# First pair of feed forward chunks multiplied with the residual stream times its channel scale, the norm factor and the shift put in behind the products

## The reference

```python
def _rmsnorm(x, g):
    xf = x.astype(jnp.float32)
    y = xf * lax.rsqrt(jnp.mean(xf * xf, axis=-1, keepdims=True) + EPS)
    return (y * g.astype(jnp.float32)).astype(x.dtype)
...
def _swiglu(h, w1, w3, w2):
    return (jax.nn.silu(h @ w1) * (h @ w3)) @ w2
...
        x = x + g1 * _mixer(h, w_in[l], b_in[l], s5_a_re[l], s5_a_im[l], s5_log_dt[l],
...
        h = _rmsnorm(x, norm2_g[l]) * (1.0 + sc2) + sh2
        x = x + g2 * _swiglu(h, ffn_w1[l], ffn_w3[l], ffn_w2[l])
```

## Time and profile before

| | us |
|---|---|
| median of 3 runs | 864.96 |
| lowest and highest run | 862.87 and 865.06 |
| the profiled execution | 865.76 |
| its span in the trace | 864.0 |
| PE busy in the span | 837.9 |
| mean granted clock | 0.991 of full speed |

### The profile page before, as it was taken

How to read it: one execution, slowest core, us unless ns; L and a number is a source line. 1 busy time by engine, 2 the same in 40 slices (tenths; PEclk the granted TensorE clock), 3 DMA queues, 4 the chain that set the end, 5 groups by cost and what they waited for, 6 DMA issues and landing times.

```text
span 864.0 us, 10537 instructions
## 1 busy us (share of the span) xinstructions
PE 837.9 (97%) x3932; PEld 677.0 (78%) x3932; DVE 442.3 (51%) x713; ACT 322.5 (37%) x475; POOL 45.6 (5%) x74
## 2 busy tenths in 40 slices
PE   6989999999999899999999999999999999999996
PEld 3668888877887677787888788888888888888886
DVE  6789876246679755326863454333333333323222
ACT  5635444433223444342334543333333332222231
POOL 5300000000000000000002100000000000000110
PEclk9999999999999999999999999999999999999999
...
GB/s 359 255 82 97 74 74 74 86 164 270 247 292 171 49 50 74 50 55 165 97 77 120 72 97 98 97 96 96 94 93 96 92 96 88 110 86 92 107 68 97
DMA packets 149372, 100.67 MB, mean 117 GB/s; under 512 B 11072, under 2 KB 142552, under 8 KB 148312
## 3 DMA queue, kind: packets, MB, share of 16 engines
...
## 4 chain that ended last, share of the span: by engine, by line
PE 87%; DVE 5%; DMA 3%; ACT 2%; issue 1%; SPq 1%; DVEq 0%; ACTq 0%
PE bank L1699 26%; PE bank L1701 25%; PE bank L1700 25%; DMA raw<-in_w_in 3%; PE bank L1846 1%; PE bank L1942 1%; PE bank L1866 1%; PE bank L1877 1%; DVE wlo L1188 1%; PE bank L1921 1%; PE bank L1967 1%; PE bank L1933 1%; ACT whi L698 1%; PE bank L1918 0%; PE bank L1818 0%
## 5 line engine op out<-in xcount | busy, mean ns | idle before, releaser
L1699 PE MATMUL bank<-h_lo,whi 128*128 128x512 f32 x712 | 286.3, 402 | 3.4 <-DVE wlo L1188 2.5
L1700 PE MATMUL bank<-h_hi,whi 128*128 128x512 f32 x712 | 279.2, 392 | 0.0
L1701 PE MATMUL bank<-h_hi,wlo 128*128 128x512 f32 x712 | 279.0, 392 | 0.0
L1699 PEld LDWEIGHTS bank<-h_lo,whi 128*128 128x128 f32 x712 | 135.0, 190 | 37.2 <-issue 6.8
L1701 PEld LDWEIGHTS bank<-h_hi,wlo 128*128 128x128 f32 x712 | 135.0, 190 | 29.1
L1700 PEld LDWEIGHTS bank<-h_hi,whi 128*128 128x128 f32 x712 | 135.1, 190 | 28.1 <-issue 1.2
L698 ACT ACTIVATE whi<-raw 128x1024 fp32r<-128x1024 f32 x60 | 63.4, 1058 | 169.5 <-PE bank L1701 124.6
L1188 DVE TENSOR_TENSOR wlo<-raw,whi 128x1024 fp32r<-128x1024 f32 x60 | 73.3, 1223 | 100.3 <-ACT whi L698 100.2
L1701 PE MATMUL bank<-a_hi,wlo 128*128 128x512 f32 x176 | 68.5, 389 | 0.0
L1699 PE MATMUL bank<-a_lo,whi 128*128 128x512 f32 x176 | 68.5, 389 | 0.0
L1700 PE MATMUL bank<-a_hi,whi 128*128 128x512 f32 x176 | 68.5, 389 | 0.0
...
## 6 DMA issues: line engine op xcount, KB each, us to landing
raw<-in_ffn_w SPq DMA_DIRECT2D x60, 512.0 KB, 3.8
raw<-in_w_in SPq DMA_DIRECT2D x44, 512.0 KB, 4.0
slab<-in_mod_w SPq DMA_DIRECT2D x32, 512.0 KB, 5.8
...
raw<-in_w_out SPq DMA_DIRECT2D x8, 512.0 KB, 3.6
...
xtok<-in_x SPq DMA_DIRECT2D x4, 512.0 KB, 5.2
```

The source lines that it names most:

```text
L1699: mm(dst, w_h, m_l, start=first, stop=False)
L1700: mm(dst, w_h, m_h, start=False, stop=False)
L1701: return mm(dst, w_l, m_h, start=False, stop=last)
```

## The change

The first pair of chunks, F0 and F1, is no longer multiplied with h2. Since h2 = (x1 * gs2) * rstd + shift, the product is W^T h2 = (W^T z) * rstd + W^T shift, with z = x1 * gs2, which needs no norm factor. So:

- ACT writes z in high part (z_hi) and in full (x1g) right behind each square, and DVE its low part (z_lo, `scaled_lo`).
- DVE makes W^T shift for F0 and F1: eight linked multiply-adds per chunk from the raw weights (sacc, `shift_times_w`), before the weights are split in place; PE sums it over partitions with a product of one column each, and DVE copies the result (bcol).
- PE multiplies F0 and F1 with z in banks 4 and 7, k by k. Both groups of `square_columns` go in after k = 2, the two shift columns and the four products that spread rstd after k = 4. All keep_clock products of this passage are gone.
- rstd is spread in bank 5 and ACT copies it to SBUF (rbs); htmp and the new zt (the pair's results times rstd) read it there. Silu gets the shift as its bias, the w3 side gets it in the product.
- F2 and F3 are multiplied as a pair, k by k, with h2, in banks 2 and 3. F3's split by ACT and DVE moves up into the loop over k. F4 to F7 are split ahead of the loops of ACT and DVE, which start one round later.

```diff
+            def scaled(n):
+                if n == 0:
+                    act.wait_ge(s_gs2, 1)
+                    act.wait_ge(s_x2t, KB)
+                    act.wait_ge(s_up, 3 * KB)
+                A(z_hi[:, n], xT[:, n], ACT.Copy, scale=gs2[:, n:n + 1]).then_inc(s_zhi, 1)
+                A(x1g[:, n], xT[:, n], ACT.Copy, scale=gs2[:, n:n + 1]).then_inc(s_x1g, 1)
...
+                act.wait_ge(s_col, n + 1)
                 if n == KB - 1:
-                    act.wait_ge(w_mm, S_F1 - 1)
-                    for s in range(S_F1, S_F1 + 2):
-                        act.wait_ge(w_loaded[s % 4], SLOT_LOADS[s])
-                        A(whi4[:, s % 4], raw[:, s % 4], ACT.Copy).then_inc(w_hi, 1)
-                act.wait_ge(s_col, n + 1)
+                    scaled(n)
                 act.wait_ge(s_sqa, n - 2)
                 A(sq[:, n % 2], xT[:, n], ACT.Square).then_inc(s_sq, 1)
-                scaled(n)
+                if n < KB - 1:
+                    scaled(n)
+                if n == KB - 3:
+                    hi4(S_F1, S_F1 - 2)
+                    hi4(S_F1 + 1, S_F1 - 1)
             act.wait_ge(s_sqmm, 1)
             A(rstd[:], ps[5][:, 0:NT], ACT.Sqrt, bias=epst[:, 0:1], scale=1.0 / D).then_inc(s_std, 1)
-
-            act.wait_ge(w_loaded[(S_F1 + 2) % 4], SLOT_LOADS[S_F1 + 2])
-            A(whi4[:, (S_F1 + 2) % 4], raw[:, (S_F1 + 2) % 4], ACT.Copy).then_inc(w_hi, 1)
+            hi4(S_F1 + 2, S_F1)
+            act.wait_ge(s_rb, 1)
+            A(rbs[:], ps[5][:], ACT.Copy).then_inc(s_rbs, 1)
             for k in range(KB):
                 b = modc[:, 24 + k:25 + k]
                 act.wait_ge(s_h2, k + 1)
                 if k in H2_POOL:
                     A(htm2[:, k % 4], htmp[:, k % 4], ACT.Identity, bias=b)
                 A(h_hi[:, k], htmp[:, k % 4], ACT.Identity, bias=b).then_inc(s_hf, 1)
-            s = S_F1 + 3
-            act.wait_ge(w_loaded[s % 4], SLOT_LOADS[s])
-            act.wait_ge(w_mm, S_F1)
-            A(whi4[:, s % 4], raw[:, s % 4], ACT.Copy).then_inc(w_hi, 1)
+                if k == 3:
+                    hi4(S_F1 + 3, S_F1)
+            for s in range(S_F1 + 4, S_F1 + 6):
+                hi4(s, s - 3)
...
+            act.wait_ge(s_zt, 1)
+            act.wait_ge(s_shb, 1)
+            A(sil[:, 0], zt[:, 0], ACT.Silu, bias=bcol[:, 0:1]).then_inc(s_sil, 1)
...
+            def scaled_lo(n):
+
+                dve.wait_ge(s_zhi, n + 1)
+                V.scalar_tensor_tensor(out=z_lo[:, n], in0=xT[:, n], scalar=gs2[:, n:n + 1],
+                                       in1=z_hi[:, n].bitcast(F32), op0=ALU.mult, op1=ALU.subtract
+                                       ).then_inc(s_zlo, 1)
...
+            def shift_times_w(w):
+
+                s = S_F1 + w
+                dve.wait_ge(w_loaded[s % 4], SLOT_LOADS[s])
+                dve.wait_ge(s_late, 3)
+                for k in range(KB):
+                    if k == 0:
+                        ins = V.tensor_scalar(sacc[:, w], raw[:, s % 4, k], modc[:, 24:25], None, ALU.mult)
+                    else:
+                        ins = V.scalar_tensor_tensor(out=sacc[:, w], in0=raw[:, s % 4, k],
+                                                     scalar=modc[:, 24 + k:25 + k], in1=sacc[:, w], op0=ALU.mult,
+                                                     op1=ALU.add)
+                    if k < KB - 1:
+                        link(ins)
+                ins.then_inc(s_shw, 1)
+
             for n in range(S_F1 - 3 - S_OUT, KB):
-                if n == KB - 1:
-                    lo4(S_F1)
-                    lo4(S_F1 + 1)
                 dve.wait_ge(w_mm, S_OUT + n + 1)
                 residual(n, n % 2, 16)
+                scaled_lo(n - 1)
+                if n == KB - 3:
+                    shift_times_w(0)
+                    dve.wait_ge(s_shw, 1)
+                    lo4(S_F1)
+                    shift_times_w(1)
+                if n == KB - 2:
+                    dve.wait_ge(s_shw, 2)
+                    lo4(S_F1 + 1)
+            scaled_lo(KB - 1)
...
-            dve.wait_ge(s_rb, 1)
+            dve.wait_ge(s_rbs, 1)
             for k in range(KB):
                 dve.wait_ge(s_x1g, k + 1)
                 if k >= 4:
                     dve.wait_ge(s_hf, k - 3)
                     dve.wait_ge(s_hlo, KB + k - 3 - sum(j <= k - 4 for j in H2_POOL))
-                V.tensor_tensor(htmp[:, k % 4], x1g[:, k], ps[3][:], ALU.mult).then_inc(s_h2, 1)
+                V.tensor_tensor(htmp[:, k % 4], x1g[:, k], rbs[:], ALU.mult).then_inc(s_h2, 1)
                 if k and k - 1 not in H2_POOL:
                     h2_lo(k - 1)
                 if k == 1:
                     lo4(S_F1 + 2)
+                if k == 4:
+                    lo4(S_F1 + 3)
+                if k == 5:
+                    dve.wait_ge(s_shc, 1)
+                    V.tensor_copy(bcol[:], ps[6][:, 0:2]).then_inc(s_shb, 1)
             h2_lo(KB - 1)
-            lo4(S_F1 + 3)
+            for w in range(2):
+                dve.wait_ge(w_mm, S_F1 + w + 1)
+                V.tensor_tensor(zt[:, w], ps[(4, 7)[w]][:], rbs[:], ALU.mult).then_inc(s_zt, 1)
+            lo4(S_F1 + 4)
+            dve.wait_ge(s_sil, 1)
+            dve.wait_ge(s_zt, 2)
+            V.scalar_tensor_tensor(out=aa[:, 0], in0=zt[:, 1], scalar=bcol[:, 1:2], in1=sil[:, 0], op0=ALU.add,
+                                   op1=ALU.mult).then_inc(s_act, 1)
+            dve.wait_ge(s_act, 3)
+            dve.wait_ge(s_ahi, 1)
+            V.tensor_tensor(a_lo[:, 0], aa[:, 0], a_hi[:, 0].bitcast(F32), ALU.subtract).then_inc(s_alo, 1)
+            lo4(S_F1 + 5)
...
-                    if n == KB - 1 and k == KB - 2:
-                        pe.wait_ge(s_x2c, KB)
-                        pe.wait_ge(s_sqa, KB - 2)
-                        square_columns(sqa, True)
                     if n == 0:
                         pe.wait_ge(s_mlo, k + 1)
                     ins = split_mm(ps[n % 2][:], whi[:, s % 3, k], wlo[:, s % 4, k], m_hi[:, k], m_lo[:, k],
                                    k == 0, k == KB - 1)
                 ins.then_inc(w_mm, 1)
-            keep_clock(3)
-            pe.wait_ge(s_sq, KB)
-            square_columns(sq[:, (KB - 1) % 2], False).then_inc(s_sqmm, 1)
-            keep_clock(1)
-            pe.wait_ge(s_rr, 1)
-            for t in range(NT):
-                ins = mm(ps[3][:, t * P:(t + 1) * P], rstd[:, t:t + 1].broadcast_to([P, P]), ident[:],
-                         start=True, stop=True)
-            ins.then_inc(s_rb, 1)
-            keep_clock(4)
-            pe.wait_ge(w_lo, S_F1 + 2)
+            for k in range(KB):
+                pe.wait_ge(s_zlo, k + 1)
+                for w in range(2):
+                    s = S_F1 + w
+                    if k == 0:
+                        pe.wait_ge(w_lo, s + 1)
+                    ins = split_mm(ps[(4, 7)[w]][:], whi4[:, s % 4, k], wlo[:, s % 4, k], z_hi[:, k], z_lo[:, k],
+                                   k == 0, k == KB - 1)
+                    if k == KB - 1:
+                        ins.then_inc(w_mm, 1)
+                if k == 2:
+                    pe.wait_ge(s_x2c, KB)
+                    pe.wait_ge(s_sqa, KB - 2)
+                    square_columns(sqa, True)
+                    pe.wait_ge(s_sq, KB)
+                    square_columns(sq[:, (KB - 1) % 2], False).then_inc(s_sqmm, 1)
+                if k == 4:
+                    pe.wait_ge(s_shw, 2)
+                    for w in range(2):
+                        ins = mm(ps[6][:, w:w + 1], sacc[:, w], ones[:, 0:1], start=True, stop=True)
+                    ins.then_inc(s_shc, 1)
+                    pe.wait_ge(s_rr, 1)
+                    for t in range(NT):
+                        ins = mm(ps[5][:, t * P:(t + 1) * P], rstd[:, t:t + 1].broadcast_to([P, P]), ident[:],
+                                 start=True, stop=True)
+                    ins.then_inc(s_rb, 1)
             for k in range(KB):
                 if k in H2_POOL:
                     pe.wait_ge(s_hlop, H2_POOL.index(k) + 1)
                 else:
                     pe.wait_ge(s_hlo, KB + k + 1 - sum(j < k for j in H2_POOL))
-                for w in range(3):
-                    s = S_F1 + w
-                    if k == 0 and w == 2:
+                for w in range(2):
+                    s = S_F1 + 2 + w
+                    if k == 0:
                         pe.wait_ge(w_lo, s + 1)
-                    ins = split_mm(ps[w][:], whi4[:, s % 4, k], wlo[:, s % 4, k], h_hi[:, k], h_lo[:, k],
+                    ins = split_mm(ps[2 + w][:], whi4[:, s % 4, k], wlo[:, s % 4, k], h_hi[:, k], h_lo[:, k],
                                    k == 0, k == KB - 1)
                     if k == KB - 1:
                         ins.then_inc(w_mm, 1)
-            s = S_F1 + 3
-            pe.wait_ge(w_lo, s + 1)
-            for k in range(KB):
-                ins = split_mm(ps[3][:], whi4[:, s % 4, k], wlo[:, s % 4, k], h_hi[:, k], h_lo[:, k],
```

(2 more changed lines are left out.)

41 lines of the change are left out of this document (33 added, 8 removed).

## The result

The changed kernel takes **869.53 us** (median of 13 runs, 867.04 to 870.57), the one before 864.96 (13 runs): ratio 1.0046, interval [1.0036, 1.0057]. So it is slower by 0.5%, a little over the 0.3% that was called no change. The forecast was 867.2 in a range of 863.8 to 869.4, with the larger chance (0.53) on no change and 0.41 on slower. The ratio on the median of before gives 864.96 x 1.0046 = 868.9, inside the range; the plain median lies 0.13 us above its end.

What follows compares the result with a forecast made beforehand. PE, 97% busy, was taken as the bound. F4 0.8 us later plus 1.4 for the clock gave +2.2 on the profiled 865.76, so 868.0; against the median, 0.8 below, 867.2 us, range 863.8 to 869.4.

Steps and rivals of the forecast that it cites:

- Stage 1: Up to the pair F0, F1: PE waits 0.9 us for F1's split, ends 0 and 2.2.
- The second hold: At F1's split: a second full hold of VectorE by GpSimd's addition of square 6, 1.30 us, in the upper end.
- rival 3: VectorE held by GpSimd at F1's split and h_lo of k = 3: +4.1 us, 869.1; 33%.
- Stage 2: First pair with its small products (squares, shift columns, factors): VectorE starts the h2 work at 496.35, 6.4 us later.
- Stage 3: Ahead of F3's first product: PE stands still 4.85 us for F3's split; F4 starts 0.8 us later than before.
- Stage 4: Granted clock falls with the wait for F3's split: 1.4 us lost, ends 0 and 1.72.
- Rival 1: As forecast, a wait for F3's split and a fallen clock: +2.2 us; 45%.
- Rival 2: The wait for F3's split comes but the clock stays: +0.8 us, 865.8; 16%.
- Rival 4: No wait at F3, its split coming before 500.3: -4.1 us, 860.9; 6%.
- After F4 nothing is late: From F4 on: VectorE's and bank 0's work is done by 512.5, ahead of F4 at 515.35, cover 2.9 us.

Runs made afterwards that it cites:

- e2: The changed kernel with the splits of F2 and F3 moved ahead of the wait for the spread norm factor: 861.44 us, ratio 0.996 to the kernel before.
- g1: The changed kernel with F3's split moved to behind h_lo of k = 1 on VectorE: 863.27 us, ratio 0.9978 to the kernel before.
- g2: The changed kernel with F3's split moved to behind htmp of k = 3 on VectorE: 862.53 us, ratio 0.9975 to the kernel before.
- e1: The changed kernel with eight keep_clock products in PE's wait for F3's split: 866.06 us, ratio 1.0009 to the kernel before.
- e3_no_shift: The changed kernel without the shift's sums and columns for F0 and F1: 866.29 us, ratio 1.0021 to the kernel before.
- a1_after: The changed kernel measured again, unedited, beside the kernel before: 869.58 us, ratio 1.0045.
- a0_after: The changed kernel measured again, unedited: 867.10 us, ratio 1.0022 to the kernel before.

## Why the prediction was right in kind and too low in size

**Stage 1.** PE was to wait 0.9 us for F1's split; it waited 0.69. The hold was forecast at 1.0: the first seven sums took 3.73 us, the second seven 2.67, so 1.06, while POOL's addition ran from 476.43 to 477.72. The second hold (upper end, and rival 3) went the other way: F1's split started at 485.59, POOL's addition at 485.76, and the split kept its 1.22 us while POOL took 2.21 instead of 1.29. The Trainium skill, "SBUF — State Buffer", section "Who interferes with whom", says that the order of issue decides who is blocked; the two rows agree. Its price for this kernel hangs on which engine starts first, and here an addition made late was off PE's path.

**Stage 2.** Squares 1.71 (forecast 1.84), shift columns 0.36 (0.45), factor products 0.90 to the next product, htmp 11.87 behind the last w_out product (forecast 496.35 - 484.32 = 12.03). F2's first product came 15.39 behind it (forecast 15.28). ACT's copy took 0.60, as taken from x1g.

**Stage 3.** From the first htmp to F3's first product: 505.85 - 497.14 = 8.71, forecast 8.8. The wait, counted like the forecast's 4.85 (from the start that was due, 501.19 + 0.23, to 505.85), is 4.43: F3's split came 0.25 earlier behind the last w_out product than forecast, and the products ahead of the wait 0.17 later. (The 4.26 of the row counts from the end of the product before.) The extra hold of h_lo of k = 3 was 0.24 (1.49 less the 1.25 of the earlier trace rows), forecast 0.4. e2, g1 and g2 show that the place of F3's split in DVE's list is what PE waits for; e1 shows that the waits alone cost +0.71 where +0.8 was forecast.

**Stage 4, the step that failed.** "I take 1.4, ends 0 and 1.72." Measured: 12.69 us from F3's first product to F4 in place of 10.2, so **2.49**, and 2.35 to 2.74 against e1_fill_wait. Both the value and its upper end were too low. The one row that I had, nine slow products behind 2.49 us of idleness, was taken as the most that could come. What it could not bound is how long the clock stays low. These are the windows in which it fell and rose again in that row of the kernel before:

```profile
62.50:63.00 0.50, 0.21 (x1) 0.22 (x2) 0.50 (x3) 0.00 (x0) 0.00 (x0) 0.95 1.13 343
...
66.00:66.50 0.50, 0.50 (x3) 0.40 (x2) 0.47 (x1) 0.00 (x0) 0.00 (x0) 0.64 0.00 0
```

Between them it was at 0.50, so it was low for 0.05 + 3.0 + 0.36 = 3.4 us, all of it behind the restart at 62.78. In the changed kernel it was low for 6.8 us, in all three profiles. I had supposed that part of the low stretch would lie inside the longer wait, and that held: 1.7, 1.1 and 1.0 us of it did. But 5.1 to 5.9 us were left for the products behind it, twelve and more in place of nine. In e3_no_shift it was again 3.4 us, behind a wait of the same 4.26.

**The sum.** Passage: the forecast's +2.2, less 0.25 for stages 1 to 3 (-0.36 from F2 to F3, +0.11 ahead of F2), plus 1.09 from F3 to F4 (12.69 against 10.2 + 1.4): +3.0, as measured. The remaining 0.95 of that pair of profiles is a later start of the passage. No part of the change is shown to cause it: a1_after has it too (0.97), while a0_after starts 1.55 earlier than before. Rival 1 is the one that happened, its clock term 1.1 us dearer. Rival 2 (the wait without the clock's fall, +0.8) is e1_fill_wait. Rival 3 named the right total (869.1) for the wrong reason: F1's split was not held at all, and the hold ahead of F3's was 0.24 in place of 1.0. Rival 4 had the right price for an earlier split but no mechanism for it; e2 is that mechanism. "After F4 nothing is late" held: the change of pace ends at F4, and the tail is within 0.06 us of before.

**What stays open.** Why the clock stayed low for 3.4 us in e3_no_shift and for 6.8 in the changed kernel behind the same 4.26 us of idleness; and what makes it fall in one execution and not in another ahead of the passage. A variant in which htmp reads the norm factor straight from PSUM, without ACT's copy and with no second SBUF input, was not tried.
